# Raw rows in the first tile behind all five norms between dense stages, squares added on GpSimd

## The reference, cut to what matters

```python
def rms_norm(x, g):
    xf = x.astype(jnp.float32)
    y = xf * lax.rsqrt(jnp.mean(xf * xf, axis=-1, keepdims=True) + EPS)
    return (y * g.astype(jnp.float32)).astype(x.dtype)

for layer in range(DEPTH):
    ...
        x = x + fox_mixer(rmsnorm(x, att_norm_g[j]), att_w_in[j], att_b_f[j], att_w_out[j])
    ...
        x = x + hgrn2_mixer(rmsnorm(x, hgrn_norm_g[j]), ...)
    x = x + conv_ffn(rmsnorm(x, ffn_norm_g[layer]), ...)
```

## Time and profile before

| | us |
|---|---|
| median of 3 runs | 3558.2 (3557.94 to 3562.71) |
| the profiled execution, its own time | 3555.62 |
| its span in the trace | 3553.8 |
| PE busy | 3379.5 (95%) |
| DVE busy | 1632.9 (46%) |
| ACT busy | 1151.5 (32%) |
| POOL busy | 84.7 (2%) |

### The profile page before, as it was taken

One profiled execution on the slowest core, in us unless ns is written; L12 is line 12 of the kernel. 1 busy time (PEld: TensorE's weight loads), 2 busy tenths in 40 slices (PEclk: granted clock), 3 DMA queues, 4 the chain that ended last, 5 costly groups with the idle time before them and its releaser, 6 DMA issues. The chain is left out here.

```text
span 3553.8 us, 41879 instructions
## 1 busy us (share of the span) xinstructions
PE 3379.5 (95%) x17392; PEld 2426.2 (68%) x17392; DVE 1632.9 (46%) x2494; ACT 1151.5 (32%) x1786; POOL 84.7 (2%) x71
## 2 busy tenths in 40 slices
PE   8989998999989989998999988998999999899998
PEld 6668875444457767876444447876888888778887
DVE  4564542211134664552111125336666664576665
ACT  5543322010034553232100114444433353543333
POOL 0000000000000000000000000000000000000000
PEclk9999998999999999998999999999999999999999
DMA  5122247999953112255999971321222222122222
GB/s 184 42 60 75 75 172 309 427 427 427 427 226 116 54 45 75 67 183 223 427 427 427 427 315 57 116 72 39 94 100 101 92 76 72 60 68 98 95 95 71
DMA packets 274939, 616.64 MB, mean 174 GB/s; under 512 B 10864, under 2 KB 210320, under 8 KB 225600
## 3 DMA queue, kind: packets, MB, share of 16 engines
q1 hardware_dynamic: 274224, 613.65, 45.5%
q10 hardware_dynamic: 528, 0.32, 0.0%
HBM read 609.71 MB, written 4.23 MB: 173 GB/s over the span
## 5 line engine op out<-in xcount | busy, mean ns | idle before, releaser
L456 PE MATMUL bank<-h_hi,w_hi 128*128 128x512 f32 x1816 | 723.3, 398 | 11.1 <-DVE w_lo L207 10.0
L458 PE MATMUL bank<-h_hi,w_lo 128*128 128x512 f32 x1816 | 710.6, 391 | 0.0
L457 PE MATMUL bank<-h_lo,w_hi 128*128 128x512 f32 x1816 | 710.3, 391 | 0.0
L207 DVE TENSOR_TENSOR w_lo<-w_raw,w_hi 128x2048 fp32r<-128x2048 f32 (+1 forms) x209 | 424.0, 2029 | 223.9 <-ACT w_hi L199 221.8
L2275 PE MATMUL bank<-expert_w,gathered 128*64 128x512 f32 x2016 | 447.1, 598 | 9.9 <-DMA expert_w<-in_w_exp_up 9.8
L199 ACT ACTIVATE w_hi<-w_raw 128x2048 fp32r<-128x2048 f32 (+1 forms) x209 | 355.4, 1700 | 229.0 <-PE bank L458 202.9
L456 PEld LDWEIGHTS bank<-h_hi,w_hi 128*128 128x128 f32 x1816 | 343.0, 189 | 99.3 <-issue 16.7
L458 PEld LDWEIGHTS bank<-h_hi,w_lo 128*128 128x128 f32 x1816 | 342.5, 189 | 73.5
L457 PEld LDWEIGHTS bank<-h_lo,w_hi 128*128 128x128 f32 x1816 | 343.2, 189 | 71.3 <-issue 1.9
L2275 PEld LDWEIGHTS bank<-expert_w,gathered 128*64 128x64 f32 x2016 | 144.1, 138 | 294.7 <-issue 288.7
L2275 PE MATMUL bank<-expert_w,hidden_t 128*64 128x512 f32 x1024 | 226.3, 595 | 0.0
(11 more groups left out here) (428 smaller groups left out, 4738.9 us busy)
## 6 DMA issues: line engine op xcount, KB each, us to landing
expert_w<-in_w_exp_up SPq DMA_DIRECT2D x64, 2048.0 KB, 21.4
expert_w<-in_w_exp_down SPq DMA_DIRECT2D x64, 2048.0 KB, 24.5
expert_w<-in_w_exp_gate SPq DMA_DIRECT2D x62, 2048.0 KB, 22.2
w_raw<-in_ffn_w_up SPq DMA_DIRECT2D x44, 1024.0 KB, 4.9
w_raw<-in_w_branch_gate SPq DMA_DIRECT2D x64, 512.0 KB, 3.8
w_raw<-in_w_in SPq DMA_DIRECT2D x22, 1024.0 KB, 5.2
w_raw<-in_ffn_w_down SPq DMA_DIRECT2D x22, 1024.0 KB, 4.8
w_raw<-in_hgrn_w_in SPq DMA_DIRECT2D x16, 1024.0 KB, 5.2
```

Of the source, the lines that this page charges most:

```text
L207: dve.tensor_tensor(self.w_lo[n % 2][:, 0:e], self.raw[n % self.RAW][:, 0:e], self.w_hi[n % 2][:, 0:e].bitcast(F32), ALU.subtract).then_in ...
L456: pe.matmul(out, st[0], mv[0], start=(j == 0), stop=False)
L457: pe.matmul(out, st[0], mv[1], start=False, stop=False)
L458: last = pe.matmul(out, st[1], mv[0], start=False, stop=(j == len(g.steps) - 1))
```

## The change

- A: the mixer's `Norm` becomes a `RawFeatureNorm`: squares and raw highs 0 to 6 and raw rests 0 to 5 in the tail, all squares added on POOL (7 adds, the last behind the barrier), sums behind kt 2, spread behind kt 4. The mixer's first two groups get banks 5 and 6.
- B: fox's `DoubleNorm` becomes a `RawDoubleNorm`: the same tail, its sums still one by one on PE, the last behind kt 1, both spreads behind kt 5. fox's first tiles become keys, queries, forget, values; its first two groups get banks 3 and 4; `forget_sums` and the second half of `gain_x` move to the turn of tile 3, and `tiles[4]` waits for them.
- C, D, E (`RawNorm`): squares and raw highs 6 and 7, all 8 raw rests and the root's table load go behind the barrier; POOL adds squares 1 to 4 in the tail and 5 to 7 behind it; PE sums one square instead of three, behind kt 5 instead of kt 1, and spreads behind kt 7 instead of kt 3.
- In all five the rest of the second tile's weights is made before the rows are scaled, not between the second and third.

```diff
-                    if kt == 1:
+                    if kt == lead.sums_row:
                         lead.sums(pe)
-                    if kt == 3:
+                    if kt == lead.spread_row:
                         lead.spread(pe)
...
+    in_tail, rests_in_tail, gathered_in_tail, sums_row, spread_row = 6, 0, 5, 5, 7
...
     def tail_act(self, act, k):
         kt = self.kt_of.get(k)
-        if kt is not None and kt < KT - 1:
+        if kt is not None and kt < self.in_tail:
             self.square(act, kt)
             self.raw_high(act, kt)
-        elif kt == KT - 1:
-            self.root_table(act)
 
     def tail_dve(self, dve, k):
         kt = self.kt_of.get(k)
-        if kt is not None and 4 <= kt < KT - 1:
-            self.raw_rest(dve, kt - 4)
+        if kt is not None and 1 <= kt <= self.rests_in_tail:
+            self.raw_rest(dve, kt - 1)
+
+    def gather_from(self, eng, first, end):
+
+        for kt in range(first, end):
+            eng.wait_ge(*self.squared(kt + 1))
+            if kt >= 2:
+                eng.wait_ge(*self.gathered_to(kt - 1))
+            eng.tensor_tensor(self.sq[:, 0, :], self.sq[:, 0, :], self.sq[:, kt, :], ALU.add).then_inc(*self.gathered.inc())
+
+    def tail_pool(self, pool):
+        self.gather_from(pool, 1, self.gathered_in_tail)
+
+    def pool_start(self, pool):
+        self.gather_from(pool, self.gathered_in_tail, KT)
+
+    def sums(self, pe):
+        pe.wait_ge(*self.gathered_to(KT - 1))
+        for tb in range(TB):
+            last = pe.matmul(self.bank[:, tb:tb + 1], self.sq[:, 0, tb * P:(tb + 1) * P], self.v.ones[:, 0:1], start=(tb == 0), stop=(tb == TB - 1))
+        last.then_inc(*self.summed.inc())
 
     def act_start(self, act):
-        self.square(act, KT - 1)
-        self.raw_high(act, KT - 1)
+        for kt in range(self.in_tail, KT):
+            self.square(act, kt)
+        for kt in range(self.in_tail, KT):
+            self.raw_high(act, kt)
+        self.root_table(act)
         self.root(act)
 
     def dve_start(self, dve):
-        for kt in range(3, KT - 1):
+        for kt in range(self.rests_in_tail, KT):
+            if kt == max(5, self.rests_in_tail):
+                self.reciprocal(dve)
             self.raw_rest(dve, kt)
-        self.reciprocal(dve)
-        self.raw_rest(dve, KT - 1)
+        self.ring.rest(dve, self.next)
...
         for kt in range(KT):
-            if kt == 2:
-                self.ring.rest(dve, self.next)
             self.scale_row(dve, kt)
...
+class RawFeatureNorm(RawNorm):
...
+    in_tail, rests_in_tail, gathered_in_tail, sums_row, spread_row = 7, 6, 7, 2, 4
...
+class RawDoubleNorm(RawNorm, DoubleNorm):
...
+    in_tail, rests_in_tail, sums_row, spread_row = 7, 6, 1, 5
...
+    def act_start(self, act):
+        self.raw_high(act, KT - 1)
+        self.root_table(act)
+        DoubleNorm.act_start(self, act)
+
+    def dve_start(self, dve):
+        self.raw_rest(dve, KT - 2)
+        DoubleNorm.dve_start(self, dve)
+        self.raw_rest(dve, KT - 1)
+        self.ring.rest(dve, self.next)
+
+    def sums(self, pe):
+        self.part(pe, KT - 1).then_inc(*self.summed.inc())
...
-    dense = Dense(v, None, tiles, banks=v.ps[0:2], ring=v.ring)
+    dense = Dense(v, None, tiles, banks=v.ps[0:2], ring=v.ring, first_banks=v.ps[5:7] if lead.raw else ())
...
+            tiles.append(Tile([(0, w_rows(w, g * 256, 256))], [features_out(v, b * P, 256, queries_to(g, b)) for b in range(2)]))
             if g == 0:
                 tiles.append(forget)
-            tiles.append(Tile([(0, w_rows(w, g * 256, 256))], [features_out(v, b * P, 256, queries_to(g, b)) for b in range(2)]))
...
-        tiles[1].pre_act, tiles[1].pre_dve = constants_r, gain(range(0, 4))
-        tiles[2].pre_act, tiles[2].pre_dve = forget_logs, gain(range(4, 8), forget_sums)
-        tiles[3].needs, tiles[4].needs = lead.x_gained.ge(8), constants.ge(2)
+        def gain(kts):
+            return lambda dve: lead.gain_x(dve, kts)
+
+        def forget_then_gain(dve):
+            forget_sums(dve)
+            lead.gain_x(dve, range(4, 8))
+
+        tiles[1].pre_act, tiles[2].pre_dve = constants_r, gain(range(0, 4))
+        tiles[3].pre_act, tiles[3].pre_dve = forget_logs, forget_then_gain
+        tiles[3].needs, tiles[4].needs = constants.ge(2), lead.x_gained.ge(8)
...
-        dense = Dense(v, None, tiles, banks=v.ps[0:3], ring=v.ring)
+        dense = Dense(v, None, tiles, banks=v.ps[0:3], ring=v.ring, first_banks=v.ps[3:5])
```

More of the change, by code:

```diff
@@ L834, in gain_x, with tail_pool, pool_start, spread @@
                                      op0=ALU.mult, op1=ALU.mult).then_inc(*self.x_gained.inc())
+class RawDoubleNorm(RawNorm, DoubleNorm):
+    in_tail, rests_in_tail, sums_row, spread_row = 7, 6, 1, 5
+    def tail_pool(self, pool):
+        pass
+    def pool_start(self, pool):
+        pass
+    def act_start(self, act):
[9 more added lines that the diff above has]
+        self.part(pe, KT - 1).then_inc(*self.summed.inc())
+    def spread(self, pe):
+        pe.wait_ge(*self.rstd.ge(1))
+        self.spread_to(pe, self.bank, self.v.rstd2)
+        self.spread_to(pe, self.v.ps[6], self.v.rstd)
 def last_norm(v, norm):
@@ L2757, in fox_first @@
 def fox_first(v):
-    return [[(0, w_rows(v.io["att_w_in_2"][0], D, 256))], [(0, w_rows(v.io["w_forget"], 0, P))]]
+    return [[(0, w_rows(v.io["att_w_in_2"][0], at, 256))] for at in (D, 0)]
 def fox(v, lead, following, next_norm):
@@ L2797, in forget_sums @@
         def forget_sums(dve):
-            dve.wait_ge(*dense.act_done(1))
+            dve.wait_ge(*dense.act_done(2))
             v.order(dve.tensor_scalar(t[0][:], t[0][:], c("b_f")[0:H, :], None, ALU.add))
@@ L2818, in fox @@
             tiles.append(Tile([(0, w_rows(w, D + g * 256, 256))], [features_out(v, b * P, 256, keys_to(g, b)) for b in range(2)]))
+            tiles.append(Tile([(0, w_rows(w, g * 256, 256))], [features_out(v, b * P, 256, queries_to(g, b)) for b in range(2)]))
             if g == 0:
                 tiles.append(forget)
-            tiles.append(Tile([(0, w_rows(w, g * 256, 256))], [features_out(v, b * P, 256, queries_to(g, b)) for b in range(2)]))
             tiles.append(Tile([(0, w_rows(w, 2 * D + g * 256, 256))], [tokens_out(v, tb, 256, 256, values_to(g, tb)) for tb in range(TB)]))
-        def gain(kts, more=None):
-            def rows(dve):
-                lead.gain_x(dve, kts)
-                if more:
-                    more(dve)
-            return rows
-        tiles[1].pre_act, tiles[1].pre_dve = constants_r, gain(range(0, 4))
-        tiles[2].pre_act, tiles[2].pre_dve = forget_logs, gain(range(4, 8), forget_sums)
-        tiles[3].needs, tiles[4].needs = lead.x_gained.ge(8), constants.ge(2)
+        def gain(kts):
[6 more added lines that the diff above has]
+        tiles[3].needs, tiles[4].needs = constants.ge(2), lead.x_gained.ge(8)
         for g in range(4):
@@ L3218, in program @@
         for turn in range(2):
-            for n in Norm.SIGNALS:
+            for n in Norm.SIGNALS + RawNorm.RAW_SIGNALS:
                 v.sig(f"{n}{turn}")
@@ L3259, in program @@
                     if last:
-                        lead = ple(v, lead, 0, fox_first(v), lambda sq, dense, groups: DoubleNorm(v, 0, v.gain_pair, sq, dense, groups))
+                        lead = ple(v, lead, 0, fox_first(v), lambda sq, dense, groups: RawDoubleNorm(v, 0, v.gain_pair, sq, dense, groups, v.layer_base + 71 * 1024, v.layer_base + 66 * 1024))
                     else:
@@ L3263, in program @@
                         following, next_gain, v.layer = mixer_first(v), v.gain("g_mix"), now
-                        lead = ple(v, lead, 1, following, lambda sq, dense, groups: Norm(v, 1, next_gain, sq, dense, groups))
+                        lead = ple(v, lead, 1, following, lambda sq, dense, groups: RawFeatureNorm(v, 1, next_gain, sq, dense, groups, v.layer_base + 71 * 1024, v.layer_base + 66 * 1024))
         assert late_base == aligned(nc.sbuf_base)
```

## The result

| | before | changed |
|---|---|---|
| median | 3557.94 (3555.92 to 3562.71, 5 runs) | 3542.11 (3541.38 to 3544.68, 5 runs) |
| profiled execution, its span | 3555.62, 3553.8 | 3542.30, 3540.5 |

The ratio is 0.9959, 95% interval 0.9946 to 0.9972: the medians lie 15.8 us apart, 3537 was forecast (21 us faster). The time lies 5 us above the forecast and inside its range of 3530 to 3549. The interval of the ratio stands for 10 to 19 us faster: that the kernel is faster is clear of the noise, and the 21 us lie just outside.

What follows compares the result with a forecast made beforehand. PE, busy 3379.5 of 3553.8 us, was taken as the bound. Gains at the five stage tops, 6.8 - 0.3 + 5.7 + 4.4 + 4.4 = 21.0 us, took the median from 3558.2 to 3537, range 3530 to 3549.

Steps and rivals of the forecast that it cites:

- C and E: First and second FFN tops: 1.2 us barrier wait, third tile at 26.2 us; gains 5.7 and 4.4 us.
- s: The start of PE behind the barrier, from which the prediction counts times at a stage top.
- D: hgrn's top: third tile waits 4.7 us behind the bounds, plus 1.5 for low clock; gains 4.4 us.
- A: Mixer norm's top: PE restarts 4.5 us behind the last matmul, not 3.0; stretch 30.3 against 37.1, gains 6.8 us.
- B: fox's top: later forget chain makes PE wait 1.9 us for x, 1.5 for second scores; loses 0.3 us.
- The sum: All five stage tops together: 21.0 us faster, with unchanged stretches taken as constant.
- 1: Rival: DVE's five rests hold back POOL's adds at the FFNs and hgrn, costing 11.4 us; time 3548.6; chance 0.13.
- 3: Rival: low-clock pieces go everywhere and hgrn's longer wait vanishes; gains 28 us, time 3530; chance 0.05.
- 2: Rival: fox gives more back, DMA collides and attention's first units run late; time 3544; chance 0.09.
- 4: Rival: PE stays at the lower clock through by-rows tiles of four stages, 18 us each; time 3607; chance 0.02.
- The rules of the skill: Rests and adds behind the barrier run one after the other; a 1.38 us table-switch drain would cost fox 1.2 us.

Runs made afterwards that it cites:

- rests_in_tail: The changed kernel with raw rests 0 to 2 back ahead of the barrier at the two FFNs and hgrn: 3544.46 us, 0.9960 of the kernel before.
- table_in_tail: The changed kernel with the root's table load back ahead of the barrier at the two FFNs and hgrn: 3543.31 us, 0.9957 of the kernel before.
- fix_d: The changed kernel with hgrn's gate bounds one tile later, behind the third tile's w_lo: 3532.97 us, 0.9928 of the kernel before.
- fix_ad: The changed kernel with hgrn's bounds one tile later and the mixer norm's raw highs moved, 6 and 7 behind the barrier: 3534.45 us, 0.9933 of the kernel before.
- fix_b: The changed kernel with fox's table load, square 7, second half of gain_x and forget rows reordered: 3538.99 us, 0.9946 of the kernel before.
- only_b: The kernel before with only fox's double norm made raw, with fox's new tile order: 3562.86 us, ratio 1.0015.

## Why the prediction was right, and where not

**C and E**: as worked out. Barrier 1.20 (1.2); sums at s+5.70 (5.5) with POOL done at s+5.16 (5.0); the third tile's rest ready at s+24.84 (24.95); PE's wait for it 0.74 (0.9); stretches 26.09 both (26.2). The stages gained 5.6 and 4.4 (5.7 and 4.4). What bounds the tops is now DVE: 25.1 of 26.1 us busy, and PE's third tile waits for its rest. rests_in_tail and table_in_tail show that both removals were needed for the 1.2: either one put back alone ends the barrier later.

**D**: wait 4.51 (4.7). The stretch, 29.9, is what was forecast without its 1.5 us for the clock (30.0); that piece came behind it, 6.8 us long from 2877.0, of which 5.0 fall on work: 2.2 us by the prediction's rate. So the stage gained 3.8 in these profiles (4.4). fix_d proves the chain named in the prediction: moved off it, the bounds give back 6.5 us in the stage.

**A**: the step that failed. "Raw high 5 (0.7) now stands on ACT ahead of the next weights' w_hi, which block 6's add follows; raw high 6 (0.7) stands ahead of the last gate ... PE restarts 4.5 us behind the last matmul instead of 3.0". The kind of delay is right and its size is not: PE restarts 5.74 behind. I added to the old end, 2.67, 1.5 us for two raw highs; but the whole tail is one chain between ACT and DVE, from block to block, and the last gate, which stood 0.57 behind the last matmul, depends through every block's square and raw high on the block ahead. The raw highs of blocks 1 and 3, 0.6 each, were left out of the sum. The last gate is at 3.17 behind the matmul, 2.6 later. The stretch took 31.8 (30.3) and the stage gained 5.0 (6.8) in the two profiles; with the A part alone the gain was 4.1. Over all profiles it is 4.0: the stage lasted 570.25 to 571.72 us in the three kernels with the old A and 566.55 to 566.98 in the ten with the new one (fix_ad's altered A left out). fix_ad shows that the 2 us by which a shorter chain moves the barrier are not had whole: more than half of them went to the low piece that begins in this wait.

**B**: forecast to lose 0.3; the stage gained 1.0 in the two profiles and 0.2 in the means of all, a wait for x of 1.29 (1.9) and one at the second scores of 0.76 (1.5), one low piece as forecast. The chain itself is as written: 5.9 us from 2230.62 to 2236.53, then `gain_x` to 2239.16. fix_b shows that the order of `gain_x` and rows is what is paid, by taking it away. What the whole-kernel runs say of B (5 us either way) stays open: much of it goes with the clock's pieces, and why these fall earlier or later in one kernel than in another I can't say.

**The sum**: 19.8 in the five stages where 21.0 was forecast, of which A is 1.8, D 0.6, C 0.1, less B's 1.3 on the other side. That these add up so well has luck in it: B's miss hides most of A's. Over all profiles with the same code in a stage (at C with only_b left out) the gains are 4.0, 0.2, 5.7, 4.4 and 4.4, together 18.7: C, D, E as forecast, B 0.5 better, A 2.8 worse. The gap that is left to the measured 15.8, 3 to 4 us, is in no term of the prediction and no larger than the noise of the comparison. The prediction took unchanged stretches as constant; in these profiles the stretch ahead of A varies by 6.7 us and the last norm by 2.3.

**The rivals.** 1 (rests hold back the adds) did not come: the adds step 1.75 us each in the mean, and end 0.5 us ahead of PE's need, but the margin is no more than that. 3 did not come: D's wait stayed, and A and D gave 5.0 and 3.8 us where it wanted 8 and 6. 2 did not come in the changed kernel, where B's waits are 1.29 and 0.76 us; in only_b the second is 1.79. 4 did not come: the clock was 1.00 in the by-rows tiles of C, D and E.

**The rules of the skill.** The five rests and three adds that start together at C take 6.53 us, where five at 0.69 and three at 1.28 (as A's lone one behind the barrier) would be 7.3 one after the other and 3.8 side by side. That is nearly one after the other, which agrees with the Trainium skill, SBUF — State Buffer, "Who interferes with whom". DVE and POOL took turns instruction by instruction (rests up to 1.79, adds up to 1.86), and neither held the other off for longer. The table load's next instruction starts 0.02 us behind it at C (2484.32 and 1.28, then 2485.62). The drain of 1.38 us that the Trainium skill, ScalarE: Activation LUTs, "What ACT_TABLE_LOAD costs", adds is not there, and the row was the better guide.

## What to carry to other kernels

Take out of the stretch ahead of a barrier whatever no one needs before it, on every engine at once: the wait ends with the last arrival, and here ACT's table, DVE's rests and POOL's fifth add each would have kept it. Behind the barrier follow the one chain to the next weights (here through DVE), and look for small work standing in it: moving the bounds of the gates, nine small DVE instructions and two tanh, was worth 6.5 us, more than A's 5.0. When moving work on a queue in a tail, walk the chain through the other engines from its first link to its end; adding the last durations to the old end is too little, as each block's share may pile up.
